# Cumulated log decays of the gated delta rule laid over all partitions by transposed columns and rows of the identity

## What is computed

```python
beta = sigmoid(b)
g = -exp(a_log) * softplus(a + dt_bias)
gcum = cumsum(chunks(g), axis=-1)
diff = gcum[..., :, None] - gcum[..., None, :]
decay = exp(where(causal, diff, -inf))
m  = where(strict, einsum('nbhik,nbhjk->nbhij', kb, kc) * decay, 0.0)
qk = einsum('nbhik,nbhjk->nbhij', qc, kc) * decay
q_dec = qc * exp(gcum)[..., None]
```

## Time and profile before

| | us |
|---|---|
| median of 3 runs | 1136.48 |
| lowest, highest | 1135.33, 1136.99 |
| the profiled execution, its own time | 1136.36 |
| span in its trace (first to last instruction) | 1134.3 |
| PE busy (share of the span) | 1106.3 (98%) |
| DVE busy | 745.1 (66%) |
| POOL busy | 516.8 (46%) |
| ACT busy | 462.4 (41%) |

### The profile page before, as it was taken

The page is one execution under the profiler, slowest core; times in us unless marked ns, Lnnn a source line. Parts: engine busy times, 40 slices in busy tenths (PEclk is TensorE's granted clock), DMA queues, the critical chain, the costliest instruction groups (busy, mean ns, idle before and its releaser), DMA issues.

```text
span 1134.3 us, 16217 instructions
## 1 busy us (share of the span) xinstructions
PE 1106.3 (98%) x5926; PEld 880.6 (78%) x5926; DVE 745.1 (66%) x964; ACT 462.4 (41%) x811; POOL 516.8 (46%) x372
## 2 busy tenths in 40 slices
PE   9998999999999999999999999999999899999996
PEld 7776888788787777777778888877778678888775
DVE  6994886416658888888861222558564867886973
ACT  6335422254753222222223334345454444244553
POOL 4554441122445545554554544433255376532533
PEclk9998999999999999999999999999999999999999
DMA  9862442151232232323233324322133122211222
GB/s 241 119 94 37 64 87 38 62 125 38 75 106 79 75 111 74 111 74 111 74 102 103 102 86 146 103 75 75 38 90 96 58 73 76 75 48 66 75 75 75
DMA packets 101722, 97.29 MB, mean 86 GB/s; under 512 B 4896, under 2 KB 95776, under 8 KB 101280
## 3 DMA queue, kind: packets, MB, share of 16 engines
q1 hardware_dynamic: 101376, 95.97, 31.1%
q10 hardware_dynamic: 288, 0.52, 0.1%
HBM read 94.38 MB, written 2.10 MB: 85 GB/s over the span
## 4 chain that ended last, share of the span: by engine, by line
PE 60%; issue 16%; DVE 11%; POOL 8%; ACT 2%; DMA 1%; POOLq 0%; DVEq 0%; SPq 0%; ACTq 0%
PE ps L1913 16%; PE ps L1915 15%; PE ps L1914 15%; POOL w_lo L538 8%; PE ps L2458 4%; DVE kq L1270 2%; PE ps L2120 1%; DVE kq L1272 1%; DVE x_a L1223 1%; DVE acc L1234 1%; DVE conv L1751 1%; PE ps L2393 1%; DVE pad L1266 1%; PE ps L2404 1%; PE ps L2305 1%
## 5 line engine op out<-in xcount | busy, mean ns | idle before, releaser
L538 POOL TENSOR_TENSOR w_lo<-raw,w_hi 128x512 fp32r<-128x512 f32 (+1 forms) x330 | 466.6, 1426 | 588.3 <-ACT w_hi L652 577.4
L652 ACT ACTIVATE w_hi<-raw 128x512 fp32r<-128x512 f32 (+1 forms) x330 | 197.0, 618 | 231.9 <-PE ps L1915 209.4
L1913 PE MATMUL ps<-x_a,w_hi 128*128 128x512 f32 x624 | 252.4, 404 | 7.4 <-issue 3.8
L1914 PE MATMUL ps<-x_a,w_hi 128*128 128x512 f32 x624 | 243.8, 391 | 0.0
L1915 PE MATMUL ps<-x_a,w_lo 128*128 128x512 f32 x624 | 243.8, 391 | 0.0
L1913 PE MATMUL ps<-x_b,w_hi 128*128 128x512 f32 x416 | 165.3, 397 | 1.7 <-POOL w_lo L538 0.8
L1915 PE MATMUL ps<-x_b,w_lo 128*128 128x512 f32 x416 | 162.3, 390 | 0.0
L1914 PE MATMUL ps<-x_b,w_hi 128*128 128x512 f32 x416 | 162.1, 390 | 0.0
L1913 PEld LDWEIGHTS ps<-x_a,w_hi 128*128 128x128 f32 x624 | 117.6, 188 | 41.2 <-issue 13.0
L1915 PEld LDWEIGHTS ps<-x_a,w_lo 128*128 128x128 f32 x624 | 117.6, 188 | 25.2
L1914 PEld LDWEIGHTS ps<-x_a,w_hi 128*128 128x128 f32 x624 | 117.7, 189 | 24.8 <-issue 2.2
(11 more groups left out here) (361 smaller groups left out, 1569.7 us busy)
## 6 DMA issues: line engine op xcount, KB each, us to landing
raw<-in_w_up SPq DMA_DIRECT2D x44, 512.0 KB, 4.4
raw<-in_w_in SPq DMA_DIRECT2D x31, 512.0 KB, 8.0
raw<-in_c_w_in SPq DMA_DIRECT2D x24, 512.0 KB, 4.6
raw<-in_a_w_in SPq DMA_DIRECT2D x18, 512.0 KB, 4.7
raw<-in_w_down SPq DMA_DIRECT2D x16, 512.0 KB, 4.1
raw<-in_w_out SPq DMA_DIRECT2D x8, 512.0 KB, 4.0
raw<-in_c_w_out SPq DMA_DIRECT2D x8, 512.0 KB, 4.1
raw<-in_w_down SPq DMA_DIRECT2D x8, 384.0 KB, 3.4
```

Of the source, the lines that this page charges most:

```text
L538: nc.gpsimd.tensor_tensor(ring_half(WL, n), raw_half(n), f32(ring_half(WH, n)), SUB) \
L652: nc.scalar.activation(ring_half(WH, n), raw_half(n), ACT.Copy).then_inc(w_hi, 1)
L1913: mm(out, w_hi_, x_hi_, start=first, stop=False)
L1914: mm(out, w_hi_, x_lo_, start=False, stop=False)
```

## The change

`T` is no longer filled with the scaled triangle. Instead, PE transposes the 128x16 columns `GC` into 16 partitions of bank 4, DVE copies them to `GCT` (the first 128 columns of the `AB` tile), and behind unit 14 sixteen products of 128 columns take the place of four of 512 columns. The weights of product `a` are the column `a` of the first 16 rows of the identity, read 128 times (a step of zero), so each product puts row `a` of `GCT` into all 128 partitions. The small product of the running sums now waits for `g` itself (`gb_ready`) and not for the scaled triangle. The transpose stands between the sums of squares of heads 1 and 2, and head 0 waits for the copy of the transposed columns.

```diff
+        GCT = AB[:, 0:P]
...
-                    v.tensor_tensor(T[:, :, :], UPPER.unsqueeze(1).broadcast_to([P, 16, P]), lastdim(GG), MUL) \
-                        .then_inc(gu_ready, 1)
                     dve.wait_ge(r4_ready, 1)
                     v.tensor_tensor(KQ[:, :, 0, :], KQ[:, :, 0, :], R4[:, :, :], MUL).then_inc(kq_normed, 1)
                 if u == 13:
                     dve.wait_ge(gc_filled, 1)
                     v.tensor_copy(GC, PS[:, 4, 0:16]).then_inc(gc_ready, 1)
+                    dve.wait_ge(gct_filled, 1)
+                    v.tensor_copy(GCT, PS[0:16, 4, P:2 * P]).then_inc(gct_ready, 1)
                     dve.wait_ge(r4_ready, 2)
...
                     if u == 13:
                         pe.wait_ge(r4_ready, 1)
-                        pe.wait_ge(gu_ready, 1)
+                        pe.wait_ge(gb_ready, 1)
                         mm(PS[:, 4, 0:16], UPPER, GG, start=True, stop=True).then_inc(gc_filled, 1)
                     for h in (1, 2, 3, 0):
+                        if h == 2 and u == 13:
+                            pe.wait_ge(gc_ready, 1)
+                            tr(PS[0:16, 4, P:2 * P], GC, IDENT[:, :]).then_inc(gct_filled, 1)
                         if h == 0 and u == 13:
-                            pe.wait_ge(gc_ready, 1)
+                            pe.wait_ge(gct_ready, 1)
                         ins = mm(PS[:, 4 + h, :], ONES[:, :], SQ4[:, h, :], start=True, stop=True)
                     ins.then_inc(ssq_filled, 1)
                 if u == 14:
 
                     pe.wait_ge(r4_ready, 2)
                     for c in range(NB):
-                        ins = mm(PS[:, 4 + c, :], ONES[:, :],
-                                 T[:, 4 * c:4 * c + 4, :].rearrange("p h i -> p (h i)"), start=True, stop=True)
+                        for h in range(H):
+                            a_ = 4 * c + h
+                            ins = mm(PS[:, 4 + c, h * P:(h + 1) * P],
+                                     IDENT[0:16, a_:a_ + 1].broadcast_to([16, P]), GCT, start=True, stop=True)
                     ins.then_inc(gcb_filled, 1)
```

More of the change, by code:

```diff
@@ L301, in build @@
         sqk, ssq_filled, r4_ready = sem("kq_squares"), sem("kq_ssq_filled"), sem("kq_norm_ready")
-        kq_normed, gu_ready = sem("kq_normed"), sem("gu_ready")
+        kq_normed, gct_filled, gct_ready = sem("kq_normed"), sem("gct_filled"), sem("gct_ready")
         gc_filled, gc_ready, lb_ready = sem("gc_filled"), sem("gc_ready"), sem("lb_ready")
```

## The result

The changed kernel is slower. Its median is 1138.66 us (19 runs, 1136.55 to 1141.56), that of the kernel before 1136.65 (19 runs beside them, 1134.47 to 1138.58): a ratio of 1.0019 with a 95% interval of 1.0011 to 1.0026, or 2.0 us. A second series gave 1138.87 (12 runs) beside 1136.13 (23 runs), ratio 1.0025, interval 1.0015 to 1.0034. The forecast was 1136.9, +0.55 us, inside a range of 1135.0 to 1138.8. The first median lies in that range, but the loss of 2.0 us in the first series and 2.7 in the second is nearly four and five times the 0.55 us of the sum.

A forecast was written before the change was run, and what follows sets the result against it. PE's own stream was taken to bound the kernel. The terms +0.11 (transpose), +0.14 (short passes) and +0.30 (changes of tile) sum to +0.55 us on 1136.36, predicting 1136.9 us, range 1135.0 to 1138.8.

The forecast's parts named there:

- What bounds the kernel: PE's own stream sets the end, so every pass added to it or taken from it should appear in the time.
- DVE's multiplication is worth nothing: Line 1420: removing its 2.23 us only adds to DVE's 4.55 us of idling for ACT's key norms; gain 0.
- The estimate for POOL's `LB`: Without DVE's multiplication beside it, LB might take 5.2 us instead of 5.53; POOL's release some 0.3 us earlier becomes idle.
- The transpose at unit 13: One added PE pass, +0.11 us; its wait for `gc_ready` is met with 0.16 us to spare.
- The products: Unit 14: 32 short passes, 3.57 us, replace 8 long ones, 3.43 us; streams alone +0.14 us.
- the changes of tile: Unit 14: PE going from 128 rows to 16 and back costs +0.30 us, bounds 0 and 0.40.
- Nothing exposed behind them: Behind the products, the ACT and DVE chain and PE's units 15 and 16 shift alike, despite 0.05 us of cover.
- Rival A: Unit 14: loads of 16-row weights not hidden behind the pass before, +3.65 us, 1140.6 us; chance 0.04.
- C: New waits not met in time, head 0's copy late: up to +0.8 us, 1137.7 us; chance 0.09.
- D: Multiplication's end matters by letting POOL and next weights come earlier: at most -0.35 us, 1136.6 us; chance 0.07.
- E: Change does less than it says, e.g. 16-row passes cost like others: +0.25, 1136.6 us; 0.78 together with the forecast.
- Rival B: 16 busy rows taken for idling, PE's clock falls, some 7 us at half clock: +3.5 us, 1140.4; chance 0.02.

The follow-up runs named there:

- the version with transposes: Changed kernel with sixteen transposes of one broadcast column replacing the products, unit 13's transpose and copy removed: 1135.46 us beside 1136.58; again 1133.62 beside 1136.13.
- the 8 products that kept the clock: Kernel before plus 8 extra products of 16 rows at each of three MLP first-projection places: 1141.81 us beside 1137.02, ratio 1.0044.
- the run with 64 rows: Kernel before plus 16 extra products of 64 rows behind each of three units of the MLP's first projection: 1147.79 us, ratio 1.0105.

## Why the prediction was wrong

- **What bounds the kernel** was right: every change of PE's stream came through whole. The distance grew by 2.25 and 2.20 us and the medians say +2.0 and +2.7; the version with transposes gained 1.67 in the stretch and 1.8 to 2.0 in the ratios.
- **DVE's multiplication is worth nothing**: right, it became idle time. The estimate for POOL's `LB` was badly off (5.2 us expected; it takes 3.61 with the multiplication gone), but the gain ended in waiting for ACT, as said:

```profile
92.72 3.61 POOL L561 TENSOR_TENSOR lb<-masks,small 128x2048 f32<-128x2048 f32 x1 [8.83 <-DVE small L1420]
96.29 1.29 POOL L539 TENSOR_TENSOR w_lo<-raw,w_hi 128x512 fp32r<-128x512 f32 x1
100.97 2.49 POOL L539 TENSOR_TENSOR w_lo<-raw,w_hi 128x512 fp32r<-128x512 f32 x2 [3.38 <-ACT w_hi L653]
```

- **The transpose at unit 13**, +0.11: measured +0.10. Its wait was met, the copy took the 0.28 us expected.
- **The products**, +0.14 and +0.30 for the changes of tile: measured +0.53 for both together. Right to 0.1 us.
- **Nothing exposed behind them**: the chain of ACT and DVE and PE shifted alike. The distance from keys by keys to keys by queries is 9.02 us (120.82 to 129.84) and was 9.03 (121.07 to 130.10).
- **Rival A** (loads of small row groups not hidden): refuted, 32 passes in 3.8 us. The rule cited with it, from the Trainium skill, "TensorE: Matmul & The Clock Gate", section "The mechanism", that a weight load overlaps a running matmul only when the row group differs, does not hold for these products: they all use the same rows, and without the changes of tile their 32 passes take 3.57 us, 0.112 each, as with 128 rows.
- **Rivals C, D and E**: the new waits cost PE nothing (the load of the transpose at 101.19 followed DVE's copy with PE still streaming), nothing was gained by POOL's earlier start, and the 16 rows did cost their changes of tile.
- **Rival B** (the clock falls) is what happened, and I gave it 0.02. This is the step that failed: the sum had no term for PE's clock behind the products, on the ground of "Against it: 8.8 us of transposes and 64-row tiles ran at 1.00". The row doesn't bear that. I took the width of the tile for the rows in use. The 64-row tiles there come in pairs, one on each half of PE's rows (the loop over `halves` in the kernel), and the 32-row tiles of the earlier trace rows come in fours, one on each quarter; neither stretch left rows unused. Two other stretches of the kernel before did. At unit 7 it is 1.4 us of one and 16 rows, shorter than even the 8 products that kept the clock. In the last level of the inverse, 32 products (lines 2166 and 2178, two passes each) use first rows 64 to 127 alone and then rows 0 to 63 alone, 3.7 us in all. The clock stays at 1.00 there, which fits the run with 64 rows and says nothing of 16 (order of time on PE, then busy time by stretch, of the kernel before):

```profile
211.54 1.90 PE L2166 MATMUL ps<-tt,m 64*64 64x64 f32 x29
...
213.46 1.85 PE L2178 MATMUL ps<-xz,t 64*64 64x64 f32 x29
```
```profile
211.50:215.30 3.80, 3.80 (x67) 3.69 (x65) 2.82 (x7) 0.48 (x2) 0.00 (x0) 1.00 0.00 0
```

So no row of the trace excluded a fall behind sixteen products of 16 rows, and 0.02 was far too little. The price was off too. It was put at 3.5 us from the stretch at 84 to 92 us; the fall was 3.4 us of half clock in both profiles (3.5 us at 0.51 in the first, 4.0 at 0.78 and 14.0 at 0.94 in the second), which costs 1.7. The missing term of 1.7 and the 0.63 measured for the rest make 2.3, which is what the distance shows (2.25 and 2.20).

The chances followed from that: nearly all weight lay on a sum whose terms were right to 0.1 us but which was not all of the time.

## What to carry over

A pass of PE cost its columns here, whatever its rows (0.112 us for 128 columns with 16 rows and with 128); but a run of products with few rows, alone on PE, can cost a second time, behind them, where other work then runs at half clock. So look in the row of a product for the rows that are in use at the same time, and if they are few in a run of products, fill them (here by copying the operand 8 times, which left 0.27 us of the 2.25) or find a form that uses all of them. And when a broadcast to all partitions is wanted, a transpose of a column read with a step of zero gives it in one pass, where a product of plain 32-bit floats takes two (1.75 us for sixteen rows, and 3.57 by products).

## What the runs showed of the hardware

- PE's granted clock fell to 0.50 while PE was busy without a break, behind 16 products (32 passes, 3.8 us) of 16 or 32 rows, and twice clearly before such a group had ended (groups of 4.47 and 4.68 us). It stayed at 1.00 behind the same products of 64 or 128 rows, and behind 8 products of 16 rows. What exactly is counted was not tried further, nor why a fall is sometimes missing or twice as long. In the profiles the fall came after 7 of 8 such groups (2 of 2 in the changed kernel, 2 of 3 with 16 rows, 3 of 3 with 32).
- Sixteen transposes with all rows in use (1.75 us) left the clock at 1.00. Whether a long run of them would was not tried.
- Going from 128 rows to 16 and back cost 0.39 us around the products (3.96 us, and 3.57 with 128 rows). To 64 rows and back it cost 0.38.
- POOL's product of `LB` went from 5.53 to 3.61 us when DVE's multiplication beside it was taken out, although both read only small tiles with steps of zero for the most part. It is 5.53 us in all six profiles with the multiplication and 3.61 in all six without it. The 1.9 us are close to the 2.23 that the multiplication took, as if one had waited for the other. No run here separates that further.
